# A transformer trunk on one core: the first norm by blocks of 128 tokens instead of columns of 128 features

## The chip, the cores and the metric

The kernel runs on one core of one Trainium2 chip. The metric is the device time of one execution in microseconds (us), the median of several runs. The engines are TensorE (PE, with its weight loads PEld), VectorE (DVE), ScalarE (ACT), GpSimd (POOL) and SyncE (SP), which issues most DMAs. Each works through its own queue in order, and they wait for one another by semaphores.

## The reference

A trunk of two pre-norm residual layers over 1024 tokens of width 1024, all in float32: layer 0 mixes tokens by an mLSTM (4 heads, chunks of 128 tokens), layer 1 by differential attention (8 heads), each is followed by a squared-ReLU MLP of width 4096, and an RMS norm ends it. The change touches only the start of layer 0:

```
def rmsnorm(x, g):
    y = x * rsqrt(mean(x * x, axis=-1) + 1e-6)
    return y * g
u = rmsnorm(x, ln_mix[0])
q, k, v, o, ig, fg = split(u @ w_in, [512, 1024, 2048, 3072, 3076])
log_i = 15 * tanh((ig + b_i) / 15)
log_f = log_sigmoid(15 * tanh((fg + b_f) / 15))
```

The kernel multiplies x by the gain first and by the reciprocal root (rstd), which belongs to a token, after the product.

## The kernel before

Activations lie with features on the 128 partitions and tokens along the free dimension: `h` is 8 feature tiles (d) of 1024 tokens, in two halves of 512. Every product of float32 is done in three matmuls of rounded parts: a value is split into `hi` (rounded) and `lo` (the rest), and PE adds hi*hi, lo*hi and hi*lo. So the input of layer 0 is made as `one` = (hi, lo), hi on ACT and lo on DVE, and each panel of 128 weight columns is split by POOL in `split` (L650 and on: hi L659, lo L664) from `w_raw` into slot 0 or 1 of `w_hi`, `w_lo`.

**The prologue, in the order of the code.** SP loads x in eight column blocks of 128 features (`load_x`, L427), each row of a block 512 bytes. PE transposes each (L977) into one of two pairs of banks of `aps` in PSUM. DVE copies the pair to `h` (L1972), ACT squares each half (L1232) and rounds gain times h to hi (L1234), DVE subtracts to give lo (L1610, semaphore `act_ready`), POOL adds the squares of the feature tiles into `acc` (L675, semaphore `x_added`). As soon as a feature tile is split, PE adds its part to the gates' product, both halves at once, in `dps[:, 0]` and `dps[:, 1]` (L992 to L994). The gates are 8 columns of `w_in`, laid in weight slot 0.

**What follows.** PE sums `acc` over the partitions with ones (L821); DVE takes the reciprocal root by ten small steps (`norm`, L1636 and L1624 to L1629); PE spreads it over the partitions (`broadcast_rstd`, L836) as a hook after four of the eight K steps of panel 1's first half; DVE copies it to `rstd_bc`. A panel is 24 matmuls for each half (L795 to L797, the same work in the loops of the heads is L813 to L815), and its result lies in `dps[:, half]` until DVE takes it out times rstd (`take`, L1646; semaphore `evac`). PE may write a bank again only after the take of what was in it. The semaphore `half_done` counts the finished half panels: 1 and 2 are the gates', 3 and 4 panel 1's. A split of panel g waits for half_done 2(g-1), as it writes the slot that panel g-2 used; the gates' slot is used again by panel 2.

**The gate chain.** DVE copies the gates' result to `g_z` (L1989), multiplies both halves by rstd (L2007), scales `gbias` (L2009, L2010), does four short steps on `lam` (L2014 to L2018), clears four tiles (L2019 to L2022) and takes panel 1. ACT does tanh, tanh, exp, ln and a scaling (L1462 to L1467). DVE then runs eight scans (L2028), L2033, and for each of eight chunks one scan (L2039) and three short steps (L2043, L2044, L2046), with the takes of panels 2 and 3 between them by a list written out by hand; then L2048 and the other takes. These are the lines of that order:

```
mlstm_takes(0, 0, 16)                      # panel 1, both halves
...                                        # eight scans, L2033
mlstm_takes(0, 16, 24)                     # panel 2, first half
for c in range(NB):
    if c in (3, 6):                        # panel 2, second half; panel 3, first half
        mlstm_takes(0, 8 * (c // 3 + 2), 8 * (c // 3 + 3))
...
mlstm_takes(0, 5 * 8, 6 * 16)              # the rest
```

SP's queue in this stretch: x block 0, the gains, the gates' weights, x blocks 1 and 2, panel 1's weights, the other x blocks, panel 2's weights (after the gates' weights are split), `hspill` (4 MB, all of h to memory, after the last lo), then the weights of the next panels.

Of the kernel before, what the change touches and what calls it, by code (L numbers as in the profile page):

```python
# [25 lines left out]
D = 1024  # L26
S = 1024
P = 128
# [4 lines left out]
MH = 4  # L33
# [72 lines left out]
def trunk(nc, x, ln_mix, ln_mlp, w_up, w_down, ln_f, m_w_in, m_b, m_norm, m_w_out,  # L106
# [82 lines left out]

    def emitted(d, half):  # L190

        return 8 * half + (4 if d < 4 else 0) + d % 4
# [14 lines left out]
    with ExitStack() as ctx:  # L207
# [133 lines left out]

        def x_bank(q):
            return aps[:, 2 * q:2 * q + 2]
# [35 lines left out]
        xt_done, xt_copied, x_added = sem("xt_done"), sem("xt_copied"), sem("x_added")  # L379
# [32 lines left out]
        def _(sp):  # L412
# [12 lines left out]
            def load_x(start, end):  # L425
                for d in range(start, end):
                    sp.dma_start(x_tok[:, :, d * P:(d + 1) * P],  # L427
                                 x_v[:, :, d * P:(d + 1) * P]).then_inc(x_ld[d], 16)
# [14 lines left out]
            load_x(1, 3)  # L443
# [28 lines left out]
            def mixer_loads(layer):  # L472
                def six(i, first=False):
                    g = G_MIX[layer] + 6 * i
                    for p in range(6):
# [20 lines left out]
                        if first and layer == 0 and p < 2:  # L496

                            if p == 1:
                                load_x(3, NT)
# [132 lines left out]
        def _(pool):  # L632
# [151 lines left out]
        def _(pe):  # L784
# [40 lines left out]
            def sum_squares(e, to=mps):  # L825

                pe.wait_ge(act_ready, 16 * (e + 1))
                if e == 0:
                    pe.wait_ge(x_added, 2 * (NT - 1))
# [138 lines left out]

            pe.wait_ge(const_ok, 4)
            for s in range(NT + 2):  # L970
                if s < NT:
                    d, b = s, 2 * (s % 2)
                    if d >= 2:
                        pe.wait_ge(xt_copied, 2 * (d - 1))
                    pe.wait_ge(x_ld[d], 16)
                    for n in range(NB):
                        last = nc.tensor.transpose(aps[:, b + n // 4, (n % 4) * P:(n % 4 + 1) * P],  # L977
                                                   x_tok[:, n, d * P:(d + 1) * P], ident[:, :])
                    last.then_inc(xt_done, 1)
                if s == 0:  # L980
                    pe.wait_ge(gain_ld, 16 * 5)
                    n_rows = 6 * NT + 1
                    nc.tensor.transpose(mps[:, 1, 0:n_rows], gain_rows,
                                        ident[0:n_rows, 0:n_rows]).then_inc(gain_done, 1)
                if s >= 2:
                    d = s - 2
                    if d == 0:
                        pe.wait_ge(gate_split, 1)
                    for half in range(2):
                        pe.wait_ge(act_ready, 2 * d + half + 1)  # L990
                        rh, rl = (piece(v, d, half) for v in one)
                        nc.tensor.matmul(dps[:, half], w_hi[:, 0, d], rh, start=(d == 0), stop=False)  # L992
                        nc.tensor.matmul(dps[:, half], w_lo[:, 0, d], rh, start=False, stop=False)
                        last = nc.tensor.matmul(dps[:, half], w_hi[:, 0, d], rl, start=False,  # L994
                                                stop=(d == NT - 1))
                        if d == NT - 1:
                            last.then_inc(half_done, 1)


            sum_squares(0)  # L1000
            half_panel(G_MIX[0], G_MIX[0] % 2, 0, *one, hook=lambda: broadcast_rstd(0))
# [212 lines left out]
        def _(act):  # L1214
# [5 lines left out]
            act.wait_ge(gain_ready, 1)  # L1220

            def emit(e, d, half, n, ready, value):
# [3 lines left out]
                if e == 0 and n >= 4:  # L1226
                    act.wait_ge(x_added, n - 3)
                elif e > 0:
                    act.wait_ge(act_ready, n - 1)
                src = h[:, d, cut]  # L1230

                last = nc.scalar.activation((acc if e == 0 and d == 0 else sq)[:, half], src, ACT.Square)  # L1232
                if e == 0:
                    last = nc.scalar.activation(piece(one[0], d, half), src, ACT.Copy,  # L1234
                                                scale=gain[:, ROW[e], d:d + 1])
                elif half == tokens(1):
# [219 lines left out]
            for d in range(NT):  # L1456
                for half in range(2):
                    emit(0, d, half, 2 * d + half, xt_copied, 2 * d + half + 1)
# [142 lines left out]
        def _(dve):  # L1601
            ch = Chain(dve, dve_chain)

            def emit(e, d, half, n):
# [3 lines left out]
                if e == 0:  # L1608

                    nc.vector.scalar_tensor_tensor(piece(one[1], d, half), h[:, d, cut], gain[:, ROW[e], d:d + 1],  # L1610
                                                   piece(one[0], d, half).bitcast(f32), ALU.mult,
                                                   ALU.subtract).then_inc(act_ready, 1)
                    return
# [20 lines left out]
            def norm(e, sums=mps):  # L1634
                dve.wait_ge(ss_done, e + 1)
                ch.link(nc.vector.tensor_scalar(small[:, 0], sums[:, 0, 0:NB], 1.0 / D, EPS, ALU.mult, ALU.add))  # L1636
# [331 lines left out]
            for s in range(NT + 1):  # L1968
                if s < NT:
                    dve.wait_ge(xt_done, s + 1)  # L1970
                    for half in range(2):
                        nc.vector.tensor_copy(h[:, s, half * HALF:(half + 1) * HALF],  # L1972
                                              aps[:, 2 * (s % 2) + half]).then_inc(xt_copied, 1)
                if s == 0:
                    dve.wait_ge(gain_done, 1)
                    nc.vector.tensor_copy(gains[:, :], mps[:, 1, 0:6 * NT + 1]).then_inc(gain_ready, 1)

                    dve.wait_ge(gate_ld, 32)
# [3 lines left out]
                    dve.wait_ge(gain_ready, 1)  # L1982
                if s >= 1:
                    for half in range(2):
                        emit(0, s - 1, half, 2 * (s - 1) + half)

            for half in range(2):
                dve.wait_ge(half_done, half + 1)
                last = nc.vector.tensor_copy(g_z[0:32 + MH, half * HALF:(half + 1) * HALF],  # L1989
                                             dps[0:32 + MH, half])  # L1990
                last.then_inc(evac, 1)
            dve.wait_ge(evac, 2)
            norm(0)
# [303 lines left out]
```

## Time and profile before

| | |
|---|---|
| median of 3 runs | 2381.99 us (2379.33 to 2382.75) |
| the profiled execution | 2383.44 us |
| its span | 2381.7 us |
| PE, DVE, ACT, POOL busy | 96%, 67%, 37%, 37% |
| mean granted PE clock | 0.984 |

Times in the profile are counted from the start of the span. A busy PE may still be at half its clock: 1.00 granted is 2.4 GHz, 0.50 is 1.2 GHz. The time of an instruction includes what it stands in execution, so a short operation with a long time was held up. Matmuls overlap: one lasts longer than the step from its start to the next one's.

### The profile page before, as it was taken

The numbers are of one execution on the slowest core, as the hardware profiler recorded it, in microseconds if no ns is written. First come the engines' busy times: TensorE is split into PE (matmuls) and PEld (weight loads), VectorE is DVE, ScalarE is ACT, GpSimd is POOL, SyncE is SP. The second block draws the span as 40 slices with busy tenths as digits, with TensorE's granted clock in tenths as the row PEclk, the third lists the DMA queues.
The fourth block names the chain that finished last, engine by engine and source line by source line (L and its number), as shares of the span: only waits on it lengthen the run. The fifth ranks groups of instructions, "written<-read, shape, count | busy, mean of one in ns | idle before, by whom it ended". The sixth has DMA issues, their size and how long they took to land.

```text
span 2381.7 us, 28693 instructions
## 1 busy us (share of the span) xinstructions
PE 2279.4 (96%) x10601; PEld 1880.6 (79%) x10601; DVE 1594.4 (67%) x1988; ACT 888.8 (37%) x1471; POOL 882.0 (37%) x672
## 2 busy tenths in 40 slices
PE   6999998899999999999899999987999999999998
PEld 5788886687888888888688888865878888888887
DVE  7534343569948749579467677775579849578396
ACT  3131122135434334344144444453145334343345
POOL 5433327410213233232476666656500233233230
PEclk9999999999999999999899999997999999999999
DMA  6111111246162442630522322212255352532601
GB/s 180 45 33 39 35 35 53 71 155 263 59 257 106 158 178 71 229 107 1 159 62 55 80 61 62 62 46 87 94 189 195 138 198 71 216 137 103 251 1 71
DMA packets 128834, 262.62 MB, mean 110 GB/s; under 512 B 7217, under 2 KB 81122, under 8 KB 121314
## 3 DMA queue, kind: packets, MB, share of 16 engines
q1 hardware_dynamic: 128290, 260.13, 32.2%
q8 instruction: 65, 1.06, 0.2%
q10 hardware_dynamic: 448, 1.18, 0.1%
q14 instruction: 31, 0.25, 0.0%
HBM read 202.56 MB, written 41.94 MB: 103 GB/s over the span
## 4 chain that ended last, share of the span: by engine, by line
PE 82%; DVE 8%; POOL 5%; ACT 2%; issue 2%; DMA 1%; SPq 0%; ACTq 0%; POOLq 0%; DVEq 0%
PE aps L913 10%; PE aps L915 9%; PE aps L917 9%; PE dps L813 6%; PE dps L815 6%; PE dps L814 5%; PE mps L913 3%; PE dps L913 3%; PE mps L915 3%; PE dps L915 3%; PE mps L917 3%; PE dps L917 3%; PE dps L795 3%; PE dps L796 3%; PE dps L797 3%; PE mps L1133 2%
## 5 line engine op out<-in xcount | busy, mean ns | idle before, releaser
L659 POOL TENSOR_TENSOR w_hi<-w_raw,ones 128x256 fp32r<-128x256 f32 (+1 forms) x127 | 175.7, 1404 | 486.9 <-PE dps L815 266.7
L813 PE MATMUL dps<-one_hi,w_hi 128*128 128x512 f32 x608 | 256.2, 421 | 1.2 <-POOL w_lo L664 1.2
L913 PE MATMUL aps<-b_ring,w_hi 128*128 128x512 f32 x640 | 249.9, 390 | 2.0 <-issue 2.0
L917 PE MATMUL aps<-b_ring,w_hi 128*128 128x512 f32 x640 | 249.0, 389 | 0.0
L915 PE MATMUL aps<-b_ring,w_lo 128*128 128x512 f32 x640 | 249.0, 389 | 0.0
L815 PE MATMUL dps<-one_lo,w_hi 128*128 128x512 f32 x608 | 238.5, 392 | 0.0
L814 PE MATMUL dps<-one_hi,w_lo 128*128 128x512 f32 x608 | 237.8, 391 | 0.0
L1708 DVE TENSOR_TENSOR b_ring<-h,b_ring 128x1024 fp32r<-128x1024 f32 x120 | 206.5, 1728 | 5.6 <-ACT b_ring L1322 5.6
L751 POOL TENSOR_TENSOR s_blk<-s_blk,a 128x1024 f32<-128x1024 f32 x24 | 68.6, 2860 | 377.6 <-DVE w_lo L1690 251.8
L664 POOL TENSOR_TENSOR w_lo<-w_raw,w_hi 128x256 fp32r<-128x256 f32 (+1 forms) x127 | 172.0, 1375 | 5.0
L795 PE MATMUL dps<-one_hi,w_hi 128*128 128x512 f32 x384 | 153.5, 400 | 11.8 <-POOL w_lo L664 4.9
L743 POOL TENSOR_TENSOR s_blk<-a,a22u 128x1024 f32<-128x1024 f32 x12 | 34.4, 2863 | 339.2 <-DMA a<-in_w_up 332.2
L913 PE MATMUL aps<-b_ring,a_hi 128*128 128x512 f32 x384 | 150.5, 392 | 5.6 <-DVE b_ring L1708 4.5
L796 PE MATMUL dps<-one_hi,w_lo 128*128 128x512 f32 x384 | 152.0, 396 | 0.0
L797 PE MATMUL dps<-one_lo,w_hi 128*128 128x512 f32 x384 | 151.6, 395 | 0.0
L915 PE MATMUL aps<-b_ring,a_lo 128*128 128x512 f32 x384 | 150.2, 391 | 0.0
L917 PE MATMUL aps<-b_ring,a_hi 128*128 128x512 f32 x384 | 150.1, 391 | 0.0
L913 PEld LDWEIGHTS aps<-b_ring,w_hi 128*128 128x128 f32 x640 | 120.1, 188 | 29.5 <-issue 4.9
L917 PEld LDWEIGHTS aps<-b_ring,w_hi 128*128 128x128 f32 x640 | 120.2, 188 | 25.2
L915 PEld LDWEIGHTS aps<-b_ring,w_lo 128*128 128x128 f32 x640 | 120.1, 188 | 24.5
L1322 ACT ACTIVATE b_ring<-h 128x1024 fp32r<-128x1024 f32 x112 | 116.5, 1048 | 49.9 <-DVE h L1743 34.9
L815 PEld LDWEIGHTS dps<-one_lo,w_hi 128*128 128x128 f32 x608 | 114.1, 188 | 25.5
(298 smaller groups left out, 5593.6 us busy)
## 6 DMA issues: line engine op xcount, KB each, us to landing
b_ring<-xs SPq DMA_DIRECT2D x42, 2048.0 KB, 7.9
xs<-b_ring SPq DMA_DIRECT2D x14, 2048.0 KB, 7.4
a<-in_w_up SPq DMA_DIRECT2D x16, 1024.0 KB, 5.4
a<-in_w_down SPq DMA_DIRECT2D x16, 1024.0 KB, 7.5
w_raw<-in_mlstm_w_in SPq DMA_DIRECT2D x24, 512.0 KB, 3.9
w_raw<-in_diff_w_in SPq DMA_DIRECT2D x24, 512.0 KB, 4.1
hspill<-h SPq DMA_DIRECT2D x2, 4096.0 KB, 12.8
h<-hspill SPq DMA_DIRECT2D x16, 512.0 KB, 3.4
```

The source lines that it names most:

```text
L659: last = nc.gpsimd.tensor_tensor(w_hi[:, slot, cut], w_raw[:, slot, cut], ones[:, :].unsqueeze(1).broadcast_to([P, piece, P]), ALU.mult)
L664: last = nc.gpsimd.tensor_tensor(w_lo[:, slot, cut], w_raw[:, slot, cut], w_hi[:, slot, cut].bitcast(f32), ALU.subtract)
L795: nc.tensor.matmul(dps[:, half], w_hi[:, slot, k], rh, start=(k == 0), stop=False)
L796: nc.tensor.matmul(dps[:, half], w_lo[:, slot, k], rh, start=False, stop=False)
L797: last = nc.tensor.matmul(dps[:, half], w_hi[:, slot, k], rl, start=False, stop=(k == NT - 1))
L813: nc.tensor.matmul(dps[:, half], w_hi[:, slot, k], rh, start=(k == 0), stop=False)
L814: nc.tensor.matmul(dps[:, half], w_lo[:, slot, k], rh, start=False, stop=False)
L815: last = nc.tensor.matmul(dps[:, half], w_hi[:, slot, k], rl, start=False, stop=(k == NT - 1))
L913: nc.tensor.matmul(to[:, n], wh, ring[:, 0, k], start=new and k == 0, stop=False, skip_group_check=not new)
L915: nc.tensor.matmul(to[:, n], wl, ring[:, 0, k], start=False, stop=False, skip_group_check=not new)
L917: last = nc.tensor.matmul(to[:, n], wh, ring[:, 1, k], start=False, stop=(k == 3), skip_group_check=not new)
L1708: last = nc.vector.tensor_tensor(lo, tiles_of(src, q), hi, ALU.subtract)
```

## The change

x is loaded in blocks of 128 tokens (n), whole rows of 4 KB, and all of the prologue goes by these blocks. PE transposes a block's eight tiles into one pair of banks. DVE multiplies the pair by the gains in one instruction of 1024, out of PSUM, into one of three buffers (`sq`, `acc`, a half of `mo`); ACT rounds that to hi in two pieces, DVE subtracts for lo in two pieces. The copy to h is done by ACT, for blocks 0 and 4 by DVE. The squares are summed by ACT's accumulator straight from the tokens, so the additions on POOL and the sum on PE fall away. The gates' product is done by halves, the first after four blocks are there; the transposes of blocks 6 and 7 stand inside it. After it come panel 1's first half, the gates' second half (with the broadcast of rstd inside), panel 1's second half. Panel 1's weights are split in pieces of 256 instead of 1024, and the split of panel 2 waits for half_done 3, now the gates' second half. half_done 1 to 4 are now gates first, panel 1 first, gates second, panel 1 second.

```diff
@@ SP
+                for n in range(start, end):
+                    sp.dma_start(x_tok[:, n], x_v[:, n]).then_inc(x_ld[n], 16)
-            load_x(1, 3)
+            load_x(1, 4)
...
-                            sp.wait_ge(act_ready, 32 * layer + 16)
+                            if layer == 0:
+                                sp.wait_ge(h_first, len(H_FIRST))
+                                sp.wait_ge(h_rest, NB - len(H_FIRST))
@@ POOL
-                    pool.wait_ge(half_done, 2 * (g - 1))
+                    pool.wait_ge(half_done, 3 if isinstance(g, int) and g == 2 else 2 * (g - 1))
-            split(1, 1, 1, first=True)
-            for n in range(2, 2 * NT):
-                pool.wait_ge(emit_hi, n + 1)
-                if n >= 4:
-                    pool.wait_ge(x_added, n - 3)
-                nc.gpsimd.tensor_tensor(acc[:, n % 2], acc[:, n % 2], sq[:, n % 2], ALU.add).then_inc(x_added, 1)
+            split(1, 1, 1, first=True, piece=PIECE)
@@ PE
+            def x_transposes(n):
+                if n >= 2:
+                    pe.wait_ge(x_scaled, n - 1)
+                    h_copied(pe, n - 2)
+                pe.wait_ge(x_ld[n], 16)
+                for d in range(NT):
+                    last = nc.tensor.transpose(x_pair(n)[:, d], x_tok[:, n, d * P:(d + 1) * P], ident[:, :])
+                last.then_inc(xt_done, 1)
+            def gate_half(half, hooks={}):
+                pe.wait_ge(act_ready, 8 * (half + 1))
+                for d in range(NT):
+                    rh, rl = (piece(v, d, half) for v in one)
...
+                    if d in hooks:
+                        hooks[d]()
+                last.then_inc(half_done, 1)
+            x_transposes(0)
...
+            for n in range(1, 6):
+                x_transposes(n)
+            pe.wait_ge(gate_split, 1)
+            gate_half(0, hooks={3: lambda: x_transposes(6), 7: lambda: x_transposes(7)})
+            half_panel(G_MIX[0], G_MIX[0] % 2, 0, *one)
+            gate_half(1, hooks={3: lambda: broadcast_rstd(0)})
             half_panel(G_MIX[0], G_MIX[0] % 2, 1, *one)
-            sum_squares(0)
@@ ACT
+            for n in range(NB):
+                act.wait_ge(x_ld[n], 16)
+                if n >= 2:
+                    act.wait_ge(x_squared, n - 1)
+                nc.scalar.activation(flat(rstd_bc[:, :, :]) if n % 2 else mo[:, 1], x_tok[:, n], ACT.Square,
+                                     accum_out=small[:, 3, n:n + 1]).then_inc(x_squared, 1)
+                act.wait_ge(x_scaled, n + 1)
+                if n not in H_FIRST:
+                    nc.scalar.activation(h[:, :, n * P:(n + 1) * P], x_pair(n), ACT.Copy).then_inc(h_rest, 1)
+                for j in range(2):
+                    nc.scalar.activation(token_piece(one[0], n, j), x_scaled_at(n)[:, 4 * j:4 * j + 4],
+                                         ACT.Copy).then_inc(emit_hi, 1)
@@ DVE
+            def x_rest(n):
+                dve.wait_ge(emit_hi, 2 * n + 2)
+                for j in range(2):
+                    nc.vector.tensor_tensor(token_piece(one[1], n, j), x_scaled_at(n)[:, 4 * j:4 * j + 4],
+                                            token_piece(one[0], n, j).bitcast(f32),
+                                            ALU.subtract).then_inc(act_ready, 1)
+            for n in range(NB):
+                dve.wait_ge(xt_done, n + 1)
+                if n >= 3:
+                    dve.wait_ge(act_ready, 2 * (n - 2))
+                nc.vector.tensor_tensor(x_scaled_at(n), x_pair(n),
+                                        gain[:, ROW[0]].unsqueeze(2).broadcast_to([P, NT, P]),
+                                        ALU.mult).then_inc(x_scaled, 1)
+                if n in H_FIRST:
+                    nc.vector.tensor_copy(h[:, :, n * P:(n + 1) * P], x_pair(n)).then_inc(h_first, 1)
...
+                if n >= 1:
+                    x_rest(n - 1)
+            x_rest(NB - 1)
+            def gate_take(half):
+                dve.wait_ge(half_done, 2 * half + 1)
+                nc.vector.tensor_copy(g_z[0:32 + MH, half * HALF:(half + 1) * HALF],
+                                      dps[0:32 + MH, half]).then_inc(evac, 1)
+            gate_take(0)
+            norm(0)
+            gate_take(1)
             dve.wait_ge(evac, 2)
-            norm(0)
```

`H_FIRST` is [0, 4]; `h_copied(eng, n)` waits for the copy of h of block n; `x_pair(n)` is the pair of banks 2(n mod 2) of `aps`; `x_scaled_at(n)` is `sq`, `acc` or `mo[:, 0]` by n mod 3; between scale 0 and scale 1 DVE splits the gates' weights, as it did before after the first copies.

## Rows read from the trace of the kernel before

**Rows 1.** The page, section 1: busy time by engine.

```profile
PE 2279.4 (96%) x10601; PEld 1880.6 (79%) x10601; DVE 1594.4 (67%) x1988; ACT 888.8 (37%) x1471; POOL 882.0 (37%) x672
```

**Rows 2.** Groups of 0 to 60 us: busy us, mean ns | idle before.

```profile
L1610 DVE SCALAR_TENSOR_TENSOR one_lo<-h,gains,one_hi 128x512 fp32r<-128x512 f32 x16 | 23.6, 1516 | 0.0
...
L675 POOL TENSOR_TENSOR acc<-acc,sq 128x512 f32<-128x512 f32 x14 | 21.9, 1584 | 2.2 <-ACT one_hi L1234 2.2
```

**Rows 3.** The timelines of PE, DVE, ACT: start, duration, what [idle before].

```profile
4.94 1.94 PE L977 MATMUL aps<-ident,x_tok 128*128 128x128 f32 x8 [4.94 <-DMA x_tok<-in_x]
...
16.70 1.04 PE L977 MATMUL aps<-ident,x_tok 128*128 128x128 f32 x8
...
43.68 0.63 PE L994 MATMUL dps<-one_lo,w_hi 128*128 128x512 f32 x1
...
55.65 1.29 DVE L2007 TENSOR_TENSOR relu<-relu,rstd_bc 36x512 f32<-36x512 f32 x2
...
57.19 1.15 ACT L1462 ACTIVATE sq<-relu,gbias 4x1024 f32<-4x1024 f32 x1 [17.46 <-DVE gbias L2010]
...
60.13 0.69 DVE L1646 SCALAR_TENSOR_TENSOR m_next<-dps,rstd_bc 128x512 f32<-128x512 f32 x1
...
62.49 0.39 PE L795 MATMUL dps<-one_hi,w_hi 128*128 128x512 f32 x1
...
64.09 5.70 DVE L2028 TENSOR_TENSOR_SCAN hn<-nm 4x128 f32<-4x128 f32 x8 [0.70 <-ACT hn L1467]
...
80.62 0.50 PE L795 MATMUL dps<-one_hi,w_hi 128*128 128x512 f32 x1 [1.64 <-DVE m_next L1646]
...
93.72 0.50 PE L795 MATMUL dps<-one_hi,w_hi 128*128 128x512 f32 x1 [1.91 <-DVE m_next L1646]
...
526.88 1.95 PE L836 MATMUL mps<-ident,rstd 128*128 128x128 f32 x16
```

**Rows 4.** The chain of waits in order of time: start, us, what.

```profile
39.42 0.43 PE dps L993
...
94.22 0.23 PE dps L796
```

**Rows 5.** Windows: length, PE busy, granted clock, DMA share, GB/s.

```profile
16.00:20.00 4.00, 2.71 (x14) 1.00 1.16 290
...
38.00:44.00 6.00, 5.37 (x12) 0.50 0.23 89
...
51.00:54.00 3.00, 3.00 (x17) 0.52 0.79 240
```

**Rows 6.** Timelines of POOL and DVE where they meet.

```profile
44.46 2.36 POOL L659 TENSOR_TENSOR w_hi<-w_raw,ones 128x1024 fp32r<-128x1024 f32 x1 [2.40 <-PE dps L994]
...
73.62 2.42 POOL L659 TENSOR_TENSOR w_hi<-w_raw,ones 128x1024 fp32r<-128x1024 f32 x1 [6.00 <-PE dps L797]
...
73.63 2.48 DVE L2044 TENSOR_SCALAR nm<-m_cur,mst 4x128 f32<-4x128 f32 x1
...
76.13 2.45 DVE L2046 TENSOR_SCALAR nm<-m_cur 4x128 f32<-4x128 f32 x1
...
78.59 0.47 DVE L2039 TENSOR_TENSOR_SCAN m_cur<-m_cur,mst 4x128 f32<-4x128 f32 x1
```

**Rows 7.** ACT's groups by form over the whole span.

```profile
L1350 ACT ACTIVATE h<-h 128x1024 f32<-128x1024 f32 x64 | 67.9, 1061 | 140.5 <-DVE h L1812 132.3 <-DVE h L1796 7.8
...
L1532 ACT ACTIVATION_READ_ACCUMULATOR ee<-aps,small 128x1 f32 x128 | 26.4, 206 | 0.0
...
L1364 ACT ACTIVATE a<-h 128x512 f32<-128x512 f32 x32 | 19.9, 622 | 22.5 <-DVE one_lo L1951 12.6 <-DVE h L1822 5.1 <-DVE acc L1947 4.8
```

**Rows 8.** DVE's groups by form over the whole span.

```profile
L1822 DVE TENSOR_TENSOR h<-h,aps 128x1024 f32<-128x1024 f32 x64 | 77.7, 1213 | 21.3 <-PE aps L917 20.8
...
L1812 DVE SCALAR_TENSOR_TENSOR h<-h,rstd_bc 128x1024 f32<-128x1024 f32 x48 | 71.6, 1491 | 0.0
...
L1646 DVE SCALAR_TENSOR_TENSOR m_next<-dps,rstd_bc 128x512 f32<-128x512 f32 x32 | 22.0, 690 | 24.2 <-PE dps L815 16.4 <-PE dps L797 7.1 <-DVE m_cur L2066 0.5
```

More of the change, by code:

```diff
@@ L188, in trunk, with h_copied @@
     ORDER = [(role, j, t) for role in (2, 1) for j in (1, 0) for t in range(4)]
+    H_FIRST = [0, 4]
+    def h_copied(eng, n):
+        if n in H_FIRST:
+            eng.wait_ge(h_first, H_FIRST.index(n) + 1)
+        else:
+            eng.wait_ge(h_rest, sum(j not in H_FIRST for j in range(n + 1)))
     def emitted(d, half):
@@ L966, in out_product @@
                     panels(g + 2 * i, g % 2, 2, *one)
-            pe.wait_ge(const_ok, 4)
[L970 to L997, printed above, removed]
@@ new lines, in gate_half @@
+            def gate_half(half, hooks={}):
+                pe.wait_ge(act_ready, 8 * (half + 1))
+                for d in range(NT):
+                    rh, rl = (piece(v, d, half) for v in one)
+                    nc.tensor.matmul(dps[:, half], w_hi[:, 0, d], rh, start=(d == 0), stop=False)
+                    nc.tensor.matmul(dps[:, half], w_lo[:, 0, d], rh, start=False, stop=False)
+                    last = nc.tensor.matmul(dps[:, half], w_hi[:, 0, d], rl, start=False, stop=(d == NT - 1))
+                    if d in hooks:
+                        hooks[d]()
+                last.then_inc(half_done, 1)
@@ new lines, in _ @@
+            pe.wait_ge(const_ok, 4)
+            x_transposes(0)
+            pe.wait_ge(gain_ld, 16 * 5)
+            n_rows = 6 * NT + 1
+            nc.tensor.transpose(mps[:, 1, 0:n_rows], gain_rows, ident[0:n_rows, 0:n_rows]).then_inc(gain_done, 1)
+            for n in range(1, 6):
[3 more added lines that the diff above has]
+            half_panel(G_MIX[0], G_MIX[0] % 2, 0, *one)
@@ L1225, in emit @@
                 act.wait_ge(ready, value)
[L1226 to L1229, printed above, removed]
+                act.wait_ge(act_ready, n - 1)
                 src = h[:, d, cut]
[L1232 to L1236, printed above, removed]
+                last = nc.scalar.activation(sq[:, half], src, ACT.Square)
+                if half == tokens(1):
                     last = nc.scalar.activation(b_ring[d // 4][:, 0, d % 4], src, ACT.Copy,
@@ L1607, in emit @@
                 dve.wait_ge(emit_hi, n + 1)
[L1608 to L1613, printed above, removed]
                 nc.vector.tensor_tensor(acc[:, half], acc[:, half], sq[:, half], ALU.add).then_inc(act_ready, 1)
@@ L1634, in norm @@
             def norm(e, sums=mps):
-                dve.wait_ge(ss_done, e + 1)
-                ch.link(nc.vector.tensor_scalar(small[:, 0], sums[:, 0, 0:NB], 1.0 / D, EPS, ALU.mult, ALU.add))
+                if e == 0:
+                    dve.wait_ge(x_squared, NB)
+                else:
+                    dve.wait_ge(ss_done, e)
+                ch.link(nc.vector.tensor_scalar(small[:, 0], small[:, 3] if e == 0 else sums[:, 0, 0:NB],
+                                                1.0 / D, EPS, ALU.mult, ALU.add))
                 rsqrt(small[:, 0], rstd[:, :], small[:, 1]).then_inc(rstd_ready, 1)
@@ L1965, in mlp @@
                     down(layer, c)
[L1968 to L1976, printed above, removed]
+            def x_rest(n):
[4 more added lines that the diff above has]
+                                            ALU.subtract).then_inc(act_ready, 1)
+            dve.wait_ge(gain_done, 1)
+            nc.vector.tensor_copy(gains[:, :], mps[:, 1, 0:6 * NT + 1]).then_inc(gain_ready, 1)
+            dve.wait_ge(gain_ready, 1)
+            for n in range(NB):
[5 more added lines that the diff above has]
+                                        ALU.mult).then_inc(x_scaled, 1)
+                if n in H_FIRST:
+                    nc.vector.tensor_copy(h[:, :, n * P:(n + 1) * P], x_pair(n)).then_inc(h_first, 1)
+                if n == 0:
                     dve.wait_ge(gate_ld, 32)
```

35 lines of the change are left out of this document (14 added, 21 removed).

## The prediction

> **What bounds the kernel now.** I read the page first: TensorE (PE) is busy 96% of the span [rows 1], so the kernel ends when PE has got through its queue, and an edit of the first 60 us counts by how much earlier or later PE enters the dense stretch that follows. I then read the groups of the first 60 us. VectorE (DVE) sets their pace: it has 16 subtractions L1610 of 1.52 us mean, slow because GpSimd (POOL) adds squares beside them, 14 times 1.58 us [rows 2]. Last, the order in time. The gates' product ends at 44.3 (last matmul 43.68, 0.63 long); panel 1, which stops for rstd on its way, gives way to panel 2 at 62.49; then the gate scans run on DVE, and PE stands 1.64 us until 80.62 and 1.91 until 93.72 for DVE's copies out of PSUM ("takes") [rows 3]. From 93.72 PE is full, so 93.72 is the mark: the forecast is where its twin lands.
>
> Two facts set prices. **The clock.** A 512-column matmul takes 0.43 us of the chain at 39.42 and 0.23 at 94.22 [rows 4]; the granted clock was 0.50 (1.2 GHz) from 38 to 44, and 0.52 from 51 to 54, when PE had stood for rstd; it was 1.00 (2.4 GHz) at 16 to 20 [rows 5]. **The lock.** A DVE instruction that reads two SBUF tensors, or a small TENSOR_SCALAR, stands until the POOL instruction beside it ends: L2044, 4x128 elements, took 2.48 us from 73.63, to the end of POOL's first pass of a weight split (73.62+2.42), and L2046 2.45 from 76.13, to the end of the second [rows 6]. The takes L1646, with one operand in PSUM, have a mean of 0.69 over 32 that meet such passes as they come [rows 8]: no lock.
>
> **The blocks.** Per block of 128 tokens ScalarE (ACT) now does: Square of 1024 (a 1024 pass in SBUF, 1.06) with an accumulator read (0.21), the copy of h (1024 again, 1.06), two roundings of 512 (0.62 each): 3.57 us [rows 7], for which I take 3.35, as back-to-back instructions start a little ahead of the end before them (two L2007 of 0.68 span 1.29 [rows 3]). DVE: scaling out of PSUM 1.2 (one PSUM operand: no lock; L1822's 1.21 [rows 8]) and two subtractions of 512, 1.3 as L2007 [rows 3], 2.5 in all, in blocks 0 and 4 also the copy of h, 1.2. PE: eight transposes, 1.94 us at 4.94 and 1.04 at 16.70, at the one clock and the other [rows 3]. So ACT sets the pace. POOL's quarters of split 1 are about 0.6 each alone, and beside blocks 0 and 1 cost DVE up to that; ACT is not waiting for it then, so nothing.
>
> PE's first transposes end at 6.88 [rows 3]; the transposed gains and their copy I put at 0.65: scale 0 ends near 8.75, block 0's roundings at 9.95. DVE then copies h (1.2) and splits the gate weights (two passes of 1024, 1.9 at most 2.4), scale 1 ends 12.9. ACT ends block 1 at 15.1, 2 at 18.45, 3 at 21.85, 4 (no copy) at 24.2, 5 at 27.6, Square 6 at 28.8. On DVE the rests of block 3 end at 23.35, and the gates' first half starts at 23.45, against 44.3 for both halves' end before. I let it start at 1.2 GHz, as PE has then had only short groups of transposes: four K steps, 12 matmuls, end about 28.2; transposes 6 at 29.2; scale 6 30.5; ACT's block 6 32.7; second four steps 32.0, transposes 7 33.1, scale 7 34.3; ACT: Square 33.9, h 35.3, roundings 36.5; rests 37.8; first gate take 38.45. PE starts panel 1's first half at 38.5, after 5.4 idle. That is a new stall: its bank is the gates' bank, and the take stands behind the rests of block 7.
>
> After such idleness I take 4.3 us at 1.2 GHz: 10 matmuls, then 14 at 0.23: 46.0. Norm 0, ten small steps, has no POOL beside it now and is done by 41. Gates' second half: 12 matmuls 2.8, the broadcast of rstd at 2.4 GHz 1.8 (as at 526.88, 1.95 with its drain [rows 3]), 12 more 2.8: it ends at T = 53.4. The matmuls that summed squares are gone. Panel 1's second half needs bank 1 taken: T+0.75, and ends at T+6.25 = 59.65, 2.8 us ahead of the 62.49 of before [rows 3].
>
> **Where that gain goes.** Split 2 waits for half_done 3 now, T, so it starts at T+0.15, as before it started 0.15 after the gates' end (44.46) [rows 6]; but before it ran beside sums and rsqrt, and now beside the multiplication of z by rstd. L2007 (two SBUF operands, 0.65 each in the clear [rows 3]) comes right after the take, T+0.7. First half: locked to the end of POOL's first pass, done T+3.05; second: locked to the end of the second, done T+5.8; gbias T+6.1 = 59.5, against 57.15 before, where ACT's tanh starts at 57.19 [rows 3]. Then L2014 and L2015 meet split 3, which waits for panel 1's end, T+6.25: one is locked for a pass. The two memsets (about 2.0 together: gbias to take was 3.0 before) I take as free; L2018 (TENSOR_SCALAR) may be locked for the second pass. Take of panel 1's first half: T+11.1 or T+13.7, before, 60.13 [rows 3]. PE, ready at 59.65, starts panel 2 at 65.25 or 67.8, before 62.49.
>
> From panel 2 to the mark are 5 half panels, 27.7 us without stalls (93.72-62.49-3.55) [rows 3]. ACT's gate chain lasts 6.9 (57.19 to the scans at 64.09 [rows 3]): scans start at 66.4, free of POOL, where before the eight took 5.70 beside split 3 [rows 3]; at 0.47 each, as L2039 [rows 6], and one pass of 1.2 they end at 71.65, where before it was 71.0. Then eight steps as before, one L2039 and three shorter, about 1.27 each, and two splits beside them that lock 4.4 each (2.48+2.45 less the work itself [rows 6]): take of panel 3's second half at 94.6. Mark: 94.65 in the first variant, 67.8+27.7 = 95.5 in the second: +0.9 or +1.8. I take +1.0: the first, nearer to the rows. Profiled execution 2383.4 (span 2381.7 and 1.7 around it), so 2384.4; it lay 1.4 over the median, which gives **2383.0 us**.
>
> **Costs at nothing.** Rows of 4 KB instead of 512 B: at 290 GB/s [rows 5] a block of 0.52 MB comes every 1.8 us and is used every 3.4; if the first came later, all would move by that. Panel 1's weights are issued on SP behind one more block, 1.8 us later, and used at 38.5. hspill is issued once all of h is copied, near 35.4, and panel 3's load stands behind it on SP: 4.2 MB at 290 GB/s is 14.5 us, so 50, and POOL wants it at 59.8. POOL's own queue is free of the additions, so nothing else stands behind its wait at T.
>
> **Unseen costs, both ends.** No row shows Square with an accumulator on 1024: 1.06 to 1.27, all ends +-1 over eight blocks; I take 1.27. Nor the scaling with a broadcast gain: 1.21 (a PSUM operand) to 1.5 (L1812's mean [rows 8]); still under ACT's 3.35, so 0 to +0.6 for the last two blocks alone. The clock: 0 us at 1.2 GHz (-4) to all of the gates' first half (+4.5). The lock at T: 0 (-2.8) to both passes and both passes of split 3 (+1.8).
>
> The Trainium skill (SBUF — State Buffer, Who interferes with whom) says the same in general form: two SBUF inputs on VectorE contend with a GpSimd instruction that reads SBUF, one input outside the two-port modes or a memset does not. By it the multiplications of z are locked and the memsets are not, and it speaks against moving the release of split 2; the trace agrees for L2044 and the takes, but shows no memset beside a POOL pass. Were memsets locked too, the mark would come out as in the second variant, +1.8.
>
> **Rivals.**
> B, the clock is up from the gates' first half on. For: 1.00 was granted from 16 to 20 with PE busy 2.71 of 4.00 us [rows 5]. Then 12 matmuls take 2.8, all later steps come 2.0 earlier, and 4.0 if panel 1 keeps it: T = 51.4 to 49.4, mark -1.1 to -3.1: 2380.
> C, the release of split 2 is harmless, because z's multiplications slip in before POOL. Against: POOL's wait and the take's end on the same matmul, and POOL was 0.15 behind it. gbias at T+2.3 = 55.7, panel 2 at 59.7: -2.8: 2379.2. With B's 4.0 as well, -6.8: 2375.2.
> D, slower: the clock stays at 1.2 GHz through the whole first half of the gates. K steps 0 to 3 end 28.6, transposes 6 (1.9) 30.5, scale 31.7, ACT 33.9, transposes 7 37.6, ACT 41.0, take 43: 4.5 later, mark +5.4: 2387.4. It is decided if matmuls stand at 0.43 at transposes 7. For: PE has had transposes only for ten us; against: eight transposes took 1.94 at 4.94 and 1.04 at 16.70, so the clock rose in a stretch that held mostly transposes [rows 3].
> The skill's TensorE: Matmul & The Clock Gate (Part 4: PE-mode transpose) says transposes do not count as activity for the full clock. By it the gates would start cold, as I assume, or stay so as in D; the trace of before speaks against it, by the two durations just given.
>
> **Chances.** Forecast 0.43; B 0.23; C 0.07; B and C together 0.13; D 0.14. A difference under 0.2%, 4.8 us, can't be told from none. Faster by more: B with C and tails of B, 0.17; slower: D and a little of the rest, 0.15; same 0.68. Range 2376.5 to 2388: it reaches B, C and D, and leaves out most of B with C.
>
> **What would show it.** ACT without a gap from block 2 to 5, about 3.4 us a block; gates' first half from 23 to 24 us; PE idle over 4 us before panel 1; z's multiplications of about 2.4 to 2.8 us each with POOL beside; panel 2's start 11 to 15 us behind the gates' second half; the stalls at 80.62 and 93.72 smaller or gone. Wrong if z's multiplications take 0.7 us, if PE starts panel 2 before 62, or if a block takes over 4 us.

## The result and the profile after

The changed kernel takes 2384.52 us (median of 20 runs, 2382.4 to 2386.94) against 2381.24 for the kernel before (20 runs, 2377.78 to 2383.37) on the same chip: a ratio of 1.0015, 95% interval [1.0008, 1.0022]. That is slower by 0.15%, inside the 0.2% that I had called "no change". The forecast was 2383.0, which is 1.0 us over the kernel before; measured are 3.3 us over it. A second timing, told below, gave 1.0003 [0.9994, 1.0012], which is 0.1 us. The profiled execution took 2383.7, its span 2381.9, where before it was 2383.44 and 2381.7.

PE is as busy as in [rows 1]; POOL has lost 20 us, DVE 9, and neither moved the end. The page of the changed kernel, section 1:

```profile
PE 2279.6 (96%) x10585; PEld 1882.1 (79%) x10585; DVE 1585.6 (67%) x1982; ACT 891.9 (37%) x1477; POOL 862.3 (36%) x664
```

The timeline of the changed kernel, its PE and ACT rows (start, duration, what, [idle before]), answers to [rows 3]:

```profile
16.99 1.05 ACT L1471 ACTIVATE rstd_bc<-x_tok 128x1024 f32<-128x1024 f32 x1
...
19.14 1.94 PE L994 MATMUL aps<-ident,x_tok 128*128 128x128 f32 x8 [1.05 <-issue]
...
19.97 1.06 ACT L1471 ACTIVATE mo<-x_tok 128x1024 f32<-128x1024 f32 x1
...
22.95 0.76 PE L1002 MATMUL dps<-one_hi,w_hi 128*128 128x512 f32 x1 [1.87 <-DVE one_lo L1990]
...
27.67 0.39 PE L1004 MATMUL dps<-one_lo,w_hi 128*128 128x512 f32 x1
...
30.23 1.03 ACT L1475 ACTIVATE h<-aps 128x1024 f32<-128x1024 f32 x1 [3.15 <-DVE sq L2001]
...
31.51 1.03 PE L994 MATMUL aps<-ident,x_tok 128*128 128x128 f32 x8
...
37.97 0.76 PE L815 MATMUL dps<-one_hi,w_hi 128*128 128x512 f32 x1 [5.42 <-DVE relu L2018]
...
58.57 1.15 ACT L1482 ACTIVATE sq<-relu,gbias 4x1024 f32<-4x1024 f32 x1 [22.67 <-DVE gbias L2041]
...
58.64 0.39 PE L817 MATMUL dps<-one_lo,w_hi 128*128 128x512 f32 x1
...
62.34 0.77 PE L815 MATMUL dps<-one_hi,w_hi 128*128 128x512 f32 x1 [3.32 <-DVE m_next L1664]
...
94.07 0.50 PE L815 MATMUL dps<-one_hi,w_hi 128*128 128x512 f32 x1 [1.38 <-DVE m_next L1664]
```

The blocks pass ACT at 2.98 us each (16.99 to 19.97). The gates' first half starts at 22.95, and PE then stands 5.42 us for the take behind block 7. The gates' chain on ACT, which started at 57.19 before, starts at 58.57. Panel 2 starts at 62.34, where it was 62.49, after a stall of 3.32. The mark, the start of the second half of panel 4, is 94.07, where it was 93.72.

DVE and POOL of the changed kernel, the same view, answer to [rows 6]:

```profile
13.16 3.69 POOL L685 TENSOR_TENSOR w_hi<-w_raw,ones 128x256 fp32r<-128x256 f32 x4 [9.86 <-DMA w_raw<-in_mlstm_w_in]
...
14.26 2.00 DVE L1990 TENSOR_TENSOR one_lo<-acc,one_hi 128x512 fp32r<-128x512 f32 x2
...
52.59 2.38 POOL L685 TENSOR_TENSOR w_hi<-w_raw,ones 128x1024 fp32r<-128x1024 f32 x1 [31.96 <-PE dps L1004]
...
53.26 5.06 DVE L2038 TENSOR_TENSOR relu<-relu,rstd_bc 36x512 f32<-36x512 f32 x2
...
58.39 0.14 DVE L2041 TENSOR_SCALAR gbias<-gbias 4x1 f32<-4x1 f32 x1
...
58.82 0.22 DVE L2046 TENSOR_TENSOR cb<-lam 128x64 f32<-128x64 f32 x1
...
59.11 2.35 POOL L685 TENSOR_TENSOR w_hi<-w_raw,ones 128x1024 fp32r<-128x1024 f32 x1 [1.34 <-PE dps L817]
...
59.29 0.14 DVE L2049 TENSOR_SCALAR again<-gains 128x1 f32<-128x1 f32 x1
...
59.59 0.91 DVE L2050 MEMSET m_cur<- 128x1024 f32 x1 [0.16 <-issue]
...
61.51 0.69 DVE L1664 SCALAR_TENSOR_TENSOR m_next<-dps,rstd_bc 128x512 f32<-128x512 f32 x1
...
65.45 2.62 DVE L2059 TENSOR_TENSOR_SCAN hn<-nm 4x128 f32<-4x128 f32 x8 [2.66 <-ACT hn L1487]
...
89.84 3.45 DVE L2079 TENSOR_TENSOR nm<-hn,m_cur 4x1024 f32<-4x1024 f32 x1
```

The two multiplications of z take 5.06 us together, where they took 1.29 [rows 3]: the first waits for the end of the POOL pass from 52.59, the second for the end of the next (57.77), and gbias is ready at 58.5. The last product with lam ends at 59.04, 0.07 before split 3. The memset from 59.59 takes 0.91 with POOL busy. The eight scans take 2.62, with no POOL pass beside them, against 5.70 [rows 3]. The take ahead of the mark stands behind L2079, which took 3.45 beside a POOL pass; its twin L2048 in the kernel before took 1.21, behind two other locked steps.

The windows of the changed kernel (window, length, busy PE, PEld, DVE, ACT, POOL, granted clock, DMA share, GB/s) answer to [rows 5]:

```profile
23.00:25.00 2.00, 2.00 (x5) 1.61 (x6) 2.00 (x3) 1.22 (x4) 0.00 (x0) 1.00 0.00 0
...
38.00:40.00 2.00, 2.00 (x5) 1.61 (x6) 1.61 (x10) 0.00 (x0) 0.00 (x0) 0.50 1.22 524
...
62.00:64.00 2.00, 1.66 (x4) 1.40 (x5) 0.80 (x2) 1.99 (x2) 1.90 (x1) 0.50 0.00 0
...
66.00:68.00 2.00, 2.00 (x6) 1.55 (x5) 2.00 (x7) 0.92 (x2) 0.00 (x0) 0.50 0.63 190
```

Panel 2 starts at 1.2 GHz (0.50) and stays there to 68. In the kernel before it ran straight on from panel 1 with matmuls 0.23 apart. The 1.00 of 23 to 25 is no proof of the high level: matmuls stand 0.43 apart there (more at the end).

### The profile page after: what moved, and what is told of

It is laid out like the page before. It is cut to its first block, busy times and chain, and to the rows that moved or that the text cites. A ratio compares the mean times of both kernels' runs of the same rounds, so it can differ in the third digit from the quotient of the medians.

```text
span 2381.9 us, 28639 instructions
## 1 busy us (share of the span) xinstructions
PE 2279.6 (96%) x10585; PEld 1882.1 (79%) x10585; DVE 1585.6 (67%) x1982; ACT 891.9 (37%) x1477; POOL 862.3 (36%) x664
## 4 chain that ended last, share of the span: by engine, by line
PE 83%; DVE 8%; POOL 5%; ACT 2%; issue 2%; DMA 1%; ACTq 0%; SPq 0%; DVEq 0%; POOLq 0%
PE aps L931 10%; PE aps L935 9%; PE aps L933 9%; PE dps L833 6%; PE dps L835 6%; PE dps L834 5%; PE mps L931 3%; PE dps L931 3%; PE dps L933 3%; PE mps L935 3%; PE mps L933 3%; PE dps L935 3%; PE dps L815 3%; PE dps L817 3%; PE dps L816 3%; PE mps L1151 2%
```

## The experiments

My theory: the input of layer 0 is split some 5 us sooner (the last rest, as I call the subtraction that gives lo, ends at 37.23 and ended at 42.61 before), and that is given back at three places. These are the order of transposes 6 and 7 (PE idle 5.4, ACT idle 3.15), the lock of z's multiplications, since split 2 is released by the same matmul as the take ahead of them, and the stall before panel 2 with the low clock behind it. Rival: the mark is set by the later splits and takes alone, so that what is done before panel 2 gains nothing. Each ratio below is to the kernel before, timed in the same set of runs; what a kernel gains on the changed kernel is read from the marks.

**1. Split 2 released behind z.**

```
     pool.wait_ge(half_done, 3 if ... g == 2 else 2 * (g - 1))
+    if g == 2: pool.wait_ge(z_ready, 2)
```

> The changed kernel, but POOL starts the split of panel 2 only after z has been multiplied by rstd (a wait for z_ready 2). Theory of the lock: in the changed kernel the two multiplications took 5.06 us beside POOL; now 1.3, so gbias is done near 54.8 instead of 58.5, the first take of panel 1 no longer holds PE for 3.3 us (at most 0.8 for the later split), and the mark (PE after the take of panel 3's second half) comes near 90 instead of 94.07: -4 us against the changed kernel, although the split itself is 2 us later. Rival (the chain behind is bound by PE's work and the takes' places, not by the lock): mark within 1 us of 94.07.

Measured: 2383.38 (11 runs), ratio 1.0004 [0.9995, 1.0013]. The gain that I expected failed to come. Its timeline, DVE, POOL and PE:

```profile
54.32 1.29 DVE L2040 TENSOR_TENSOR relu<-relu,rstd_bc 36x512 f32<-36x512 f32 x2
...
55.78 2.42 POOL L687 TENSOR_TENSOR w_hi<-w_raw,ones 128x1024 fp32r<-128x1024 f32 x1 [35.28 <-DVE relu L2040]
...
55.85 2.43 DVE L2047 TENSOR_TENSOR cb<-lam 128x64 f32<-128x64 f32 x1
...
58.31 2.43 DVE L2048 TENSOR_TENSOR cb<-lam 128x64 f32<-128x64 f32 x1
...
60.61 2.35 POOL L687 TENSOR_TENSOR w_hi<-w_raw,ones 128x1024 fp32r<-128x1024 f32 x1
...
64.03 0.77 PE L817 MATMUL dps<-one_hi,w_hi 128*128 128x512 f32 x1 [3.96 <-DVE m_next L1666]
```

z is free (1.29), but the products with lam, 0.23 each in the changed kernel, are caught instead, 2.43 each, and split 3 stands right behind. (Ahead of z all of this trace is about a microsecond later than in the changed kernel: in its gates' first half all 12 matmuls of the first four K steps stood 0.43 apart, and in panel 1 nine instead of seven.) PE stalls 3.96 us before panel 2, and the mark is 95.65. The lock moved to the next instructions with two SBUF operands; it was not removed. So the lock of z is real, but releasing POOL later is no remedy for it.

**2. All transposes first.**

```
-    for n in range(1, 6):
+    for n in range(1, NB):
...
-    gate_half(0, hooks={3: ...x_transposes(6), 7: ...x_transposes(7)})
+    gate_half(0)
```

> The changed kernel, but the transposes of blocks 6 and 7 stand ahead of the gates' first half instead of inside it. Theory (their place makes ACT wait 3.15 us for block 6 and PE 5.4 us before panel 1): ACT's block 6 follows without the gap, last rest near 33.7 instead of 37.2, gates' first half from about 27 to 35, panel 1 from about 35.8 instead of 37.97 with PE idle about 1 us, so the gates' second half ends near 49 instead of 52.4 and the mark near 90.6. Rival (the clock, low after a longer stretch of transposes alone, eats it): gates' first half all at 0.43 a matmul, 27 to 37.5, panel 1 from 38.3: mark 94 or later.

Measured: 2377.75 (11 runs), ratio 0.998 [0.9971, 0.9989]; span 2374.9, mark 88.52. Its timeline, PE and DVE:

```profile
25.04 1.94 PE L994 MATMUL aps<-ident,x_tok 128*128 128x128 f32 x8 [1.45 <-issue]
...
31.98 1.29 DVE L1990 TENSOR_TENSOR one_lo<-acc,one_hi 128x512 fp32r<-128x512 f32 x2 [1.69 <-ACT one_hi L1477]
...
35.18 0.47 PE L815 MATMUL dps<-one_hi,w_hi 128*128 128x512 f32 x1 [0.87 <-DVE relu L2018]
...
48.96 5.06 DVE L2038 TENSOR_TENSOR relu<-relu,rstd_bc 36x512 f32<-36x512 f32 x2
...
58.05 0.74 PE L815 MATMUL dps<-one_hi,w_hi 128*128 128x512 f32 x1 [3.32 <-DVE m_next L1664]
```

The last rests start at 31.98, against 35.94 in the changed kernel, and PE idles 0.87 instead of 5.42 before panel 1. The lock of z (5.06) and the stall of 3.32 are still there, only earlier. The rival falls: PE went into panel 2 4.3 us sooner (58.05 against 62.34), and the mark came 5.55 sooner (94.07 - 88.52). The other 1.3 us is the clock: behind the same stall of 3.32 eight matmuls stood 0.43 apart here, and 14 in the changed kernel.

**3. Gates together.** The second half of the gates right behind the first, panel 1 whole behind both.

```
-    half_panel(G_MIX[0], G_MIX[0] % 2, 0, *one)
-    gate_half(1, hooks={3: lambda: broadcast_rstd(0)})
+    gate_half(1)
+    half_panel(G_MIX[0], G_MIX[0] % 2, 0, *one, hook=lambda: broadcast_rstd(0))
...
-    dve.wait_ge(half_done, 2 * half + 1)
+    dve.wait_ge(half_done, half + 1)
```

and split 2 waits for half_done 2.

> The changed kernel, but the gates' second half is done right after the first, and panel 1 whole after it with the broadcast of rstd in its first half (the split of panel 2 again waits for half_done 2). Theory: PE still stands about 5 us for block 7, but no longer for the take; gates done near 44.4, split 2 runs from there beside nothing that it locks, z is multiplied near 52 in 1.3 us, PE goes into panel 2 at about 57.2 instead of 62.3 and the mark is near 88: -6 us against the changed kernel, about -5 against before. Rival (the order of halves was worth its cost): no gain, 94 or more.

Measured: 2379.17 (11 runs), ratio 0.9986 [0.9977, 0.9995]; mark 88.59. Its timeline, PE, POOL and DVE:

```profile
37.48 0.50 PE L1002 MATMUL dps<-one_hi,w_hi 128*128 128x512 f32 x1 [4.74 <-DVE one_lo L1990]
...
44.99 2.40 POOL L685 TENSOR_TENSOR w_hi<-w_raw,ones 128x1024 fp32r<-128x1024 f32 x1 [24.25 <-PE dps L1004]
...
51.42 1.28 DVE L2038 TENSOR_TENSOR relu<-relu,rstd_bc 36x512 f32<-36x512 f32 x2
...
75.50 0.50 PE L815 MATMUL dps<-one_hi,w_hi 128*128 128x512 f32 x1 [1.64 <-DVE m_next L1664]
```

Split 2 runs from 44.99 to 49.83 and is over before z is multiplied; z takes 1.28, and PE goes into panel 2 without a stall. So an earlier release did what the later one of experiment 1 didn't. The stalls of before return (1.64 at 75.50, 1.92 at 88.59): the later splits bound again.

**4. Both (2 and 3).**

> Both edits: all transposes first, both gate halves together, then panel 1. Theory: gates from about 27 to 40, panel 2 from about 53, mark near 84: -10 us against the changed kernel, -9.5 against before (near 2372). Rival: the two gains overlap, as both remove the same idleness of PE before panel 1; then the mark is that of the better one, 88.

Measured: 2373.13 (5 runs), ratio 0.996 [0.9947, 0.9974]; mark 83.02, span 2369.9. Against the changed kernel's mark, 2 gives 5.55, 3 gives 5.48 and both give 11.05. So the gains do not overlap, as the rival had it. That they add up so exactly is partly luck of the clock: in this trace the gates' first half ran at 2.4 GHz from its first matmul, where nine matmuls stood 0.43 apart in kernel 2 and eleven in kernel 3.

**5. Quarters.** The changed kernel with splits 2 to 4 in passes of 256 instead of 1024 columns. (The expectation speaks of panels 2 and 3; the kernel quarters split 4 as well.)

```
-    split(2, 0, 1)
+    split(2, 0, 1, piece=PIECE)
...
-    pairs(3, G_OUT[0])
+    split(3, 1, 2, piece=PIECE)
+    split(4, 0, 2, piece=PIECE)
+    pairs(5, G_OUT[0])
```

> The changed kernel, but the splits of panels 2 and 3 in pieces of 256, so that a locked VectorE instruction waits for at most one piece (about 0.6 us) and not for a pass of 2.4. The wait added before (split 2 after z) only moved the lock from z to the two products of lam, 2.43 us each. If the lock is what holds back the take of panel 1 and so PE (3.3 us idle, then a low clock in panel 2): z's two multiplications together about 2.5 us instead of 5.06, take of panel 1 near 59.5 to 60.5 instead of 61.5, PE into panel 2 at about 60.3 or before instead of 62.34 and at the full clock, mark near 90 instead of 94.07 (-4 us). Rival (the pieces together lock as long as the two passes, each of them once, and POOL gets slower): z's products about 5 us again, mark 94.

Measured: 2381.08 (11 runs), ratio 0.9992 [0.9983, 1.0001]; mark 90.20, span 2379.9. Its timeline, POOL, DVE and PE:

```profile
53.56 3.79 POOL L685 TENSOR_TENSOR w_hi<-w_raw,ones 128x256 fp32r<-128x256 f32 x4 [33.05 <-PE dps L1006]
...
54.23 1.83 DVE L2040 TENSOR_TENSOR relu<-relu,rstd_bc 36x512 f32<-36x512 f32 x2
...
56.78 0.66 DVE L2048 TENSOR_TENSOR cb<-lam 128x64 f32<-128x64 f32 x1
...
60.73 0.47 PE L817 MATMUL dps<-one_hi,w_hi 128*128 128x512 f32 x1 [0.75 <-DVE m_next L1666]
...
83.17 2.19 DVE L2076 TENSOR_TENSOR mst<-m_cur,hn 4x1 f32<-4x1 f32 x1
...
85.39 2.51 DVE L2077 TENSOR_SCALAR nm<-m_cur,mst 4x128 f32<-4x128 f32 x1
...
90.20 0.68 PE L817 MATMUL dps<-one_hi,w_hi 128*128 128x512 f32 x1 [2.01 <-DVE m_next L1666]
```

z takes 1.83, the locked product 0.66, PE idles 0.75 instead of 3.32 before panel 2 and starts it at the full clock. So one lock lasts as long as one POOL instruction, and no longer. Split 5, uncut, still locks 2.19 and 2.51 and gives a stall of 2.01 with the clock low behind it. The mark is 3.9 us earlier, although the trace was a microsecond late ahead of z, as in experiment 1; the span is only 2.0 shorter.

**6. Both with quarters**: kernel 4 with splits 2 to 6 in quarters.

> The kernel with all transposes first and both gate halves together, whose mark came at 83.02 with PE idle 1.65 and 1.92 us for takes held up by locked steps of the gate chain; here the splits of panels 2 to 6 go in pieces of 256. If locks set those takes: the steps of the gate chain beside a split cost at most 0.6 us extra each, both stalls of PE go or shrink under 1 us together, mark 79.5 to 80.5, time 2370 (-3 against that kernel, -12 against before). Rival: eight small locks cost what two large ones did, or pieces on POOL (0.8 us beside VectorE) delay the splits beyond PE's need: mark 83 or later.

Measured: 2371.61 (5 runs), ratio 0.9952 [0.9938, 0.9965]; span 2364.7. Its timeline, PE, POOL and DVE:

```profile
54.96 5.12 DVE L2063 TENSOR_TENSOR_SCAN hn<-nm 4x128 f32<-4x128 f32 x8 [1.59 <-ACT hn L1491]
...
69.54 0.51 PE L819 MATMUL dps<-one_hi,w_hi 128*128 128x512 f32 x1 [0.58 <-DVE m_next L1668]
...
75.46 2.82 POOL L685 TENSOR_TENSOR w_hi<-w_raw,ones 128x256 fp32r<-128x256 f32 x4 [6.08 <-PE dps L821]
...
76.24 0.73 DVE L2079 TENSOR_SCALAR nm<-m_cur,mst 4x128 f32<-4x128 f32 x1
```

A locked step takes 0.73 instead of 2.5; of the two stalls one of 0.58 is left, and PE runs through the mark at 80.59 without a stop, 2.4 us sooner than in kernel 4. But the pieces lock more steps than two long passes did: the eight scans took 5.12 beside split 3, where kernel 4's took 4.81 beside the uncut split and the changed kernel's 2.62 in the clear. Where every step of a chain can be locked, quarters gain little; here they gain because the takes that PE waits for come sooner.

**7. The kernel before with quarters alone** (splits 2 to 6, nothing of the change).

> The kernel before, with the splits of panels 2 to 6 in pieces of 256 and nothing else changed. Lock theory: the locked steps of the gate chain (2.48 and 2.45 beside split 4, the same beside split 5) shrink to 0.7 each, the two stalls of PE (1.64 and 1.91) go down to about 0.6 together, mark 93.72 - 3 = 90.7, time 3 us under before. Rival: the smaller pieces hold up as much in sum, mark 93 or later, same time.

Measured: 2379.53 (11 runs), ratio 0.9987 [0.9978, 0.9996]; mark 89.48. Its timeline, DVE and PE:

```profile
86.20 0.69 DVE L2050 TENSOR_SCALAR nm<-m_cur 4x128 f32<-4x128 f32 x1
...
89.48 0.50 PE L799 MATMUL dps<-one_hi,w_hi 128*128 128x512 f32 x1 [0.33 <-DVE m_next L1650]
```

So the lock costs the kernel before as well: the stall at 80.62 is gone and the one ahead of the mark is 0.33 instead of 1.91, 3.2 us together; the median is 3.3 lower. The mark came 4.2 sooner, but 0.7 of that was there before panel 2. The eight scans were no faster for it (5.93 beside the quarters of split 3, 5.70 in [rows 3]).

**8. All mLSTM splits in quarters** on top of kernel 6 (`pairs(7, G_OUT[0], PIECE)`).

> The kernel with transposes first, gates together and quarters for panels 2 to 6, now with quarters for all panels of the mLSTM. If locks cost PE in the heads too (it waits 2.7 us for the copy to sq and 2.3 for cb per head), time 2368 to 2370 instead of 2371.6; if the slower POOL (5.7 us a split instead of 4.9) or nothing there matters, 2371 to 2373.

Measured: 2368.44 (5 runs), ratio 0.9945 [0.9932, 0.9959]: the fastest version, 0.55% or some 13 us under before. The intervals of kernels 6 and 8 overlap: what the further quarters add is not resolved. PE ran through the mark at 79.77 without a stop.

**9. How far the 3.3 us between the medians is real**: the changed kernel profiled again, before profiled twice more, and the changed kernel timed again.

> The changed kernel once more, for a second trace. The trace of before has its mark at 93.72 and that of the changed kernel at 94.07, 0.35 apart, but the medians of 20 runs are 3.3 us apart. If the mark varies with where the clock falls: it will lie elsewhere than 94.07 by 1 us or more. If not, within 0.5 and the 3.3 us arise behind the mark.

> The kernel before once more, for a second trace. Its profiled execution (2383.44) was slower than 19 of its 20 timed runs (median 2381.24). If the prologue is what varies, the mark lies 2 us or more before 93.72; if it is the stretch behind, the mark is within 0.5 of it and the span shorter.

> The changed kernel again, timed beside the kernel before. Its mark came at 94.07 and 93.66 in two traces, that of before at 93.72 and 93.75, so up to the mark the two are equal. If the 3.3 us between the medians of 20 runs are real, they lie behind the mark and come again here: ratio 1.0008 to 1.0022, about 2 to 5 us slower. If they were chance of that set, the ratio here is within 0.0005 of 1.

> The kernel before for a third trace: mark within 0.1 of 93.7 as in the other two, span between 2376 and 2382; the stretch behind the mark is what varies (2288.0 and 2288.1 so far).

Measured: after, profiled again, 2383.22 (span 2381.4, mark 93.66); after timed again 2382.97 (11 runs) against 2382.87, ratio 1.0003 [0.9994, 1.0012] (mark 93.46, span 2377.7); before 2383.72 (span 2381.9, mark 93.75) and 2382.3 (span 2380.5, mark 91.99). In that last one the clock did not fall while PE stood for rstd; its timeline, PE:

```profile
50.66 2.05 PE L836 MATMUL aps<-ident,rstd 128*128 128x128 f32 x16 [1.92 <-DVE rstd L1629]
```

Sixteen transposes took 2.05 there. So two of my expectations failed: the third trace of before has its mark 1.7 us ahead of 93.7, where I had allowed 0.1, and the span of the second, 2381.9, is no shorter than that of the first. Mark and span don't go together closely: the span less the mark is 2288.0, 2288.2 and 2288.5 in three traces of before, 2287.8, 2287.7 and 2284.2 in three of after, and 2286.3 to 2290.2 in kernels 1 to 5, though nearly all of the code there is the same.

The runs come from several sets, and the median of the kernel before differs between them: 2381.24 in the first, 2382.15 beside kernels 1 to 6, 2382.87 beside kernels 7 and 8 and the second timing of after. So the table is to be compared by its ratios, not by its medians.

| kernel | mark | span | median | ratio to before |
|---|---|---|---|---|
| before | 93.72 | 2381.7 | 2381.24 | 1 |
| after | 94.07 | 2381.9 | 2384.52 | 1.0015 [1.0008, 1.0022] |
| after, timed again | 93.46 | 2377.7 | 2382.97 | 1.0003 [0.9994, 1.0012] |
| 1 split 2 behind z | 95.65 | 2381.9 | 2383.38 | 1.0004 [0.9995, 1.0013] |
| 2 transposes first | 88.52 | 2374.9 | 2377.75 | 0.998 [0.9971, 0.9989] |
| 3 gates together | 88.59 | 2378.8 | 2379.17 | 0.9986 [0.9977, 0.9995] |
| 4 both | 83.02 | 2369.9 | 2373.13 | 0.996 [0.9947, 0.9974] |
| 5 quarters | 90.20 | 2379.9 | 2381.08 | 0.9992 [0.9983, 1.0001] |
| 6 both, quarters | 80.59 | 2364.7 | 2371.61 | 0.9952 [0.9938, 0.9965] |
| 7 before, quarters | 89.48 | 2374.3 | 2379.53 | 0.9987 [0.9978, 0.9996] |
| 8 all quarters | 79.77 | 2366.6 | 2368.44 | 0.9945 [0.9932, 0.9959] |

## Why the prediction was right

The mechanism held: what the prologue won was given back before the mark. Step by step, forecast and measured:

- **Blocks.** Forecast 3.35 us each, measured 2.98: a mis-sized term. Square (1.05) and the read (0.20) took what I had taken for them, but I had taken off only 0.22 for the overlap. Each of the five instructions starts about 0.1 ahead of the end before it, so that durations of 3.42 in sum pass in 2.98. The gates' half won only 0.5 us by it, because ACT did not set its start, as I had said: DVE did. DVE ran without a gap from 6.66 to 25.15 and ended block 3's rests at 22.81, 2.7 us after ACT had rounded that block (20.08). And POOL's quarters of split 1, which I had put at nothing, locked two pairs of rests: 2.00 and 2.02 us instead of 1.28.
- **Gates' first half.** Start 23.45, measured 22.95, at 1.2 GHz as assumed, up at 27.4. **Idle before panel 1** 5.4, measured 5.42, for the reason named; experiment 2 confirms it. Panel 1's 1.2 GHz lasted 3.2 us, not 4.3. **T** 53.4, measured 52.44 (52.05 + 0.39).
- **Lock of z.** Forecast to the end of both passes, gbias at T+6.1 = 59.5; measured 5.06 us and T+6.1 = 58.5. Experiments 1 and 3 show the cause by its absence (1.29 and 1.28 with no pass beside), experiment 5 by shorter passes (1.83).
- **Lam and the memsets.** I let one product be locked for a pass of split 3. Measured: both slipped by with 0.07 us to spare, and nothing behind them was locked; the memsets are free. Panel 2 started at T+9.9, not T+11.85, and outside the 11 to 15 us that I had named as a sign. This term failed by 1.95. In the third trace PE even entered panel 2 at 61.84, under the 62 that I had named as a sign of being wrong, with the lock and the stall of 3.32 as in the others.
- **Panel 2 to the mark.** Here lies what the sum didn't have: after the stall of 3.32 the clock was low, and panel 2's first half lasted 8.4 us (62.34 to 70.77) instead of 5.4, so +3.0. I had counted the clock after the idleness before panel 1, and not after the one that I forecast myself (5.6 us, from 59.65 to 65.25). In return the stall at 80.62 is gone, and that before the mark is 1.38 instead of 1.91. Mark 94.65 forecast, 94.07 measured. The closeness is partly luck, as errors of both signs cancel: -1.0 at T, -1.95 at lam, +2.3 behind it (31.7 us against 29.4).
- **Scans.** 3.8 forecast, 2.62 measured, 0.33 each.
- **Nothing for the memory.** No wait for data inside the dense part; hspill was issued at 34.95 (35.4 forecast); the takes and POOL never waited for weights there.

Rival B (clock up from the gates on) falls in all three traces of after: the first matmuls of the gates stand 0.43 apart. Rival C falls: z was locked. Rival D falls: the clock rose between 26.4 and 27.7, before transposes 6 were through. The transposes' durations separate B and D better than the clock column does. Of the pages: the Trainium skill (TensorE: Matmul & The Clock Gate, Part 4: PE-mode transpose) doesn't count transposes as activity for the full clock, and I had held the trace of before against it. That was a weak argument: ahead of the group of 1.04 at 16.70 [rows 3] PE had done six matmuls of 512 columns there, the first at 13.22. In the changed kernel the 48 transposes before 21.1 us bear the page out: four groups of eight took 1.94 each and one of sixteen 3.67. But in kernel 4 a group took 1.07 at 25.22, with only transposes ahead of it, so it isn't without exception; its timeline, PE:

```profile
25.22 1.07 PE L994 MATMUL aps<-ident,x_tok 128*128 128x128 f32 x8 [1.47 <-issue]
```

The other one, the Trainium skill (SBUF — State Buffer, Who interferes with whom), held for the memset, which no row of before showed: 0.91 beside a pass of POOL.

**Open.** The first timing has after slower by 3.3 us, the second by 0.1; both intervals hold 1.0008 to 1.0012, 2 to 3 us. At the mark the three traces of after lie -0.3 to +0.35 from the two of before in which the clock fell at rstd, and 1.5 to 2.1 behind the one in which it didn't. How often it does is not known from three traces. What differs behind the mark (by up to 4 us between executions of the same code) I can't place; whether the change costs nothing or 3 us isn't settled.

## What to carry to other kernels

A release of GpSimd that is tied to the same event as a VectorE chain with two SBUF operands puts the lock on that chain. Releasing it a little later moves the lock to the next instructions; releasing it early enough to be over before the chain begins removes it (experiments 1 and 3). Shorter GpSimd instructions shrink each wait, but lock more instructions. Short work that starts another engine's chain (transposes 6 and 7 here, for which ACT waited 3.15 us) belongs ahead of a long phase of TensorE and not inside it, when a take stands behind that chain. And an idle time of TensorE is priced with the low clock that can follow: behind the 3.32 us it cost another 3.0 us in the changed kernel and 1.7 in kernel 2.

## What the runs showed of the hardware

- In these traces the granted-clock column reads 1.00 until its first recorded fall, at whichever level PE runs. In the changed kernel it reads 1.00 at 23 to 25 with matmuls 0.43 apart; in kernel 1 one group of transposes took 1.07 at 13.12, the column then showed a fall, and reads 0.50 beside groups of the same 1.94. Its windows:

```profile
16.00:20.00 4.00, 2.84 (x13) 2.50 (x14) 4.00 (x5) 4.00 (x9) 3.92 (x5) 0.50 0.79 252
```

  So early in a program the durations tell the clock, not the column; my case for rival B rested on that column.
- A locked step waits for one GpSimd instruction, not for a burst: it took 2.43 beside a pass of 1024 columns, 0.66 to 0.73 beside one of 256. The next step can be locked again: eight scans took 5.12 beside quarters. A TENSOR_SCALAR of 128x1 went through in 0.14 beside POOL (59.29), while one of 4x128 is locked.
- Behind a stall of 3.3 us before panel 2 the clock was at 1.2 GHz for some 6 us in the changed kernel and 3.5 us in kernel 2; behind single stalls of 0.75 (kernel 5) and 0.87 (kernel 2) it stayed up. But the low stretch from 38 to 44 in [rows 5] came after stalls of 0.7 to 1.1 each, one after every few matmuls. So the length of the last stall alone doesn't tell what the clock will do. Around 2 us it went either way in the same code: sixteen transposes behind PE's wait for rstd took 2.05 in one execution of before, and in the one of [rows 5] the clock read 0.52 there.
